# Turning the last context tile in the middle of the second chunk of the second layer's input stage

## The reference

```python
h = rmsnorm(x, p["g_pre_mix"]) * (1 + sc1) + sh1
hc = rmsnorm(xc, p["g_pre_mix"]) * (1 + sc1c) + sh1c
u = h @ w_in
if last:
    uc_mla_kv = hc @ w_in[:, MLA_Q_END:MLA_KV_END]
    uc_na_kv = hc @ w_in[:, NA_Q_END:]
...
y_cf = conformer_conv_mixer(u[..., MLA_KV_END:CF_END], ...)
```

## Time and profile before

| | us |
|---|---|
| median of 3 runs | 1428.51 (1427.56 to 1429.23) |
| the profiled execution | 1429.31 |
| its span, first to last instruction | 1427.4 |
| TensorE busy | 1388.3 (97% of the span) |
| VectorE, ScalarE, GpSimd busy | 994.5, 672.1, 83.3 |
| mean granted TensorE clock | 0.998 of full speed |

### The profile page before, as it was taken

How to read it: one execution, slowest core, us unless ns; L and a number is a source line. 1 busy time by engine, 2 the same in 40 slices (tenths; PEclk the granted TensorE clock), 3 DMA queues, 4 the chain that set the end, 5 groups by cost and what they waited for, 6 DMA issues and landing times.

```text
span 1427.4 us, 21688 instructions
## 1 busy us (share of the span) xinstructions
PE 1388.3 (97%) x8558; PEld 1188.3 (83%) x8558; DVE 994.5 (70%) x1507; ACT 672.1 (47%) x1057; POOL 83.3 (6%) x125
## 2 busy tenths in 40 slices
PE   6999999999999999999999999999999999999998
PEld 3787657888888888788868899888998999899996
DVE  3777477567776856678785765567897556786867
ACT  4421366651231313456266644466545664654544
POOL 0000000010001111100000360000000000000000
PEclk9999999999999999999999999999999999999999
DMA  9422460343645647436322455555545434455453
GB/s 384 192 74 74 177 237 31 140 170 107 233 163 200 227 162 287 155 118 215 116 73 99 169 190 192 180 201 197 175 178 177 153 129 169 156 178 186 169 207 118
DMA packets 39510, 241.06 MB, mean 169 GB/s; under 512 B 4496, under 2 KB 4928, under 8 KB 15488
## 3 DMA queue, kind: packets, MB, share of 16 engines
q1 hardware_dynamic: 28624, 198.92, 38.3%
q0 software_dynamic: 10800, 40.92, 8.2%
HBM read 238.75 MB, written 1.07 MB: 168 GB/s over the span
## 4 chain that ended last, share of the span: by engine, by line
PE 86%; DVE 5%; DMA 4%; ACT 4%; issue 1%; SPq 0%; DVEq 0%; ACTq 0%; POOLq 0%
PE ps L662 44%; PE ps L711 17%; PE ps L743 5%; DMA w<-in_stream 3%; PE ps L630 2%; PE ps L682 2%; PE ps L771 2%; DVE w_lo L486 2%; PE ps L1159 1%; PE ps L799 1%; PE ps L1039 1%; PE ps L1192 1%; DMA U<-in_start 1%; ACT w_hi L476 1%; PE ps L854 1%
## 5 line engine op out<-in xcount | busy, mean ns | idle before, releaser
L662 PE MATMUL ps<-h_hi,w_hi 128*128 128x256 f32 (+1 forms) x1488 | 464.3, 312 | 2.6 <-DVE w_lo L486 1.4
L662 PE MATMUL ps<-h_hi,w_lo 128*128 128x256 f32 (+1 forms) x1488 | 460.2, 309 | 0.0
L662 PE MATMUL ps<-h_lo,w_hi 128*128 128x256 f32 (+1 forms) x1488 | 460.1, 309 | 0.0
L486 DVE TENSOR_TENSOR w_lo<-w,w_hi 128x1024 fp32r<-128x1024 f32 x332 | 393.1, 1227 | 73.4 <-ACT w_hi L476 69.3
L476 ACT ACTIVATE w_hi<-w 128x1024 fp32r<-128x1024 f32 x332 | 333.0, 1053 | 226.6 <-DMA w<-in_stream 226.5
L662 PEld LDWEIGHTS ps<-h_hi,w_hi 128*128 128x128 f32 x1488 | 283.9, 191 | 20.4 <-issue 3.7
L662 PEld LDWEIGHTS ps<-h_lo,w_hi 128*128 128x128 f32 x1488 | 283.9, 191 | 14.9 <-issue 0.5
L662 PEld LDWEIGHTS ps<-h_hi,w_lo 128*128 128x128 f32 x1488 | 283.8, 191 | 14.6
L711 PE MATMUL ps<-w_hi,g_hi 128*128 128x512 f32 x344 | 134.9, 392 | 1.7 <-DVE w_lo L486 1.0
L711 PE MATMUL ps<-w_hi,g_lo 128*128 128x512 f32 x344 | 133.9, 389 | 0.0
L711 PE MATMUL ps<-w_lo,g_hi 128*128 128x512 f32 x344 | 133.9, 389 | 0.0
(11 more groups left out here) (336 smaller groups left out, 1962.6 us busy)
## 6 DMA issues: line engine op xcount, KB each, us to landing
w<-in_stream SPq DMA_DIRECT2D x176, 1024.0 KB, 4.8
hf<-in_mod_blocks POOLq DMA_DIRECT2D x38, 512.0 KB, 4.2
SW<-in_mod_blocks POOLq DMA_DIRECT2D x18, 512.0 KB, 4.9
U<-in_start SPq DMA_DIRECT2D x4, 1024.0 KB, 16.0
GA<-gates POOLq DMA_DIRECT2D x6, 512.0 KB, 4.7
w<-in_start SPq DMA_DIRECT2D x2, 1024.0 KB, 9.8
w<-in_stream SPq DMA_DIRECT2D x4, 512.0 KB, 7.3
GA<-in_start SPq DMA_DIRECT2D x2, 1024.0 KB, 10.9
```

The lines of the kernel that those rows point to most:

```text
L486: dve.tensor_tensor(k.w_lo[:, c.slot, half], k.w[:, c.slot, half], k.w_hi[:, c.slot, half].bitcast(f32), ALU.subtract).then_inc(k.lo_done, 1)
L662: last = pe.matmul(k.banks(2 * c.pair, n, j * (512 if tiles == 2 else n)), w[a][:, c.slot, at:at + 128], h[b][:, kt * stride:kt * stride + n],
```

## The change

In the second layer alone, the turning of tile 3 is taken from between chunk 0 and chunk 1 and is made the `middle` of chunk 1, between its first 24 and its last 24 matmuls.

```diff
     middle = {4: latent_squares, 9: lambda: scores(1)}
+    if l == 1:
+        middle[1] = lambda: pe_tile(k, pe, "mix1", 3)
...
             to_features(k, pe, At(c0 + j), h, KT, 256, 2, n, NT_ALL, before_kt=tokens_ready.get(j), middle=middle.get(j))
-        if l == 1 and j == 0:
-            pe_tile(k, pe, "mix1", 3)
         if j in after:
             after[j]()
```

## The result

The changed kernel takes 1433.67 us (median of 12 runs, 1431.67 to 1436.98), the kernel before 1428.62 us (12 runs, 1427.44 to 1430.83). The ratio is 1.0033, with a 95% interval from 1.0026 to 1.0041: slower by 5 us, and the whole interval is above the 0.2% that the prediction took as its line. The forecast was 1431.6 us in a range from 1429.4 to 1433.9; the measured time is in the range, and 0.4 us from what the clock rival gave (1433.3). It is 2.1 us above the forecast itself.

A forecast was written before the change was run, and what follows sets the result against it. TensorE, 86% of the chain, bounds the kernel. Chunk 2 starts 3.05 us late (0.95 us transposes, 2.10 us new wait), so the median goes from 1428.51 to about 1431.6 us; range 1429.4 to 1433.9 us.

The forecast's parts named there:

- the clock rival: TensorE's idle stretches of 2.61 and 2.1 us halve its clock, up to 1.7 us more: 1433.3 us; chance 0.20.
- Part 1: Chunk 1's first matmul still waits for `w_lo` from VectorE; two waits become one of 2.61 us; gain 0.
- Part 2: Transposes inside chunk 1 lose their cover and take 0.95 us of TensorE's time among dense matmuls.
- The sum: Span 1427.4 + 3.05 = 1430.45 us; median of the runs from 1428.51 to 1431.56, say 1431.6 us (+0.21%).
- Part 3: ScalarE's and VectorE's work queued behind the turned tile makes chunk 2 start at 654.52, not 651.47: +3.05 us.
- Part 4: After chunk 2 no later wait up to 735 us absorbs the delay, so nothing gives the 3 us back.
- the likeliest case: The forecast itself, 1431.6 us from chunk 2's start 3.05 us later; chance 0.56.

The follow-up runs named there:

- e6: Changed kernel with the first half of chunk 1's `w_lo` made ahead of the norm of tile 3; 1432.68 us, ratio 1.0025 to the kernel before.
- e5: Changed kernel, chunk 0's take and chunk 2's weight split put ahead of tile 3's work on ScalarE and VectorE, idle stretch before chunk 1 filled; 1430.14 us, ratio 1.0010.
- e4: Kernel before, transposes in their old place, only the signal to ScalarE moved to after the 24th matmul of chunk 1; 1433.24 us, ratio 1.0030.
- e2: Changed kernel with unused transposes filling TensorE's idle stretches, 20 ahead of chunk 1 and 16 ahead of chunk 2; 1432.90 us, ratio 1.0028.
- e1: The changed kernel run once more with nothing filled; 1436.03 us, ratio 1.0038 to the kernel before.
- e3: Changed kernel with only the idle stretch ahead of chunk 1 filled, by 20 unused transposes; 1433.25 us, ratio 1.0030.
- e8: Changed kernel with only the idle stretch ahead of chunk 2 filled, by 16 unused transposes; 1433.76 us, ratio 1.0029.
- e7: Changed kernel, chunk 1's weights split ahead of tile 3's norm, chunk 2's split and chunk 0's take ahead of tile 3's reads, nothing filled; 1428.09 us, ratio 0.9994.
- e12: Version of e7 with ten unused transposes right ahead of the first layer's 1.46 us wait; 1426.41 us, ratio 0.9979 to the kernel before.
- e10: Changed kernel with both idle stretches filled and ten unused transposes in the first layer, one step behind its wait; 1433.27 us, ratio 1.0032.

## Why the prediction was right, and where it was not

**Part 1 (chunk 1's start does not move): right.** The wait was 2.52 us (2.61 expected), released by `w_lo`, and e6 shows that this `w_lo` was its cause.

**Part 2 (0.95 us for the transposes): right in size, wrong as a term of a sum.** e5 measures 0.86 us. But e4 shows that taking them off the path doesn't save them: the start of chunk 2 moves by 2.58 us with them covered (e4) and by 3.09 with them in the chain (e2). The step of the prediction that wrote the 3.05 as "0.95 is the work of the transposes and 2.10 a new wait" is right as a description of TensorE's time and misleading as a price list. The sum itself was not made that way, but along the chain, and held.

**Part 3 (chunk 2 starts 3.05 us later): right.** At full clock (e2) it was 3.09, with ScalarE idle for 5.03 us ahead of its reads, where about 5 was forecast. The lag from VectorE's first half of `w_lo` to TensorE was 1.47 us in the changed kernel in place of the 1.36 taken from chunk 1.

**Part 4 (it stays): right.** L1105 had no wait, VectorE's idle time behind it was 2.51 us (2.48 in rows 7), and at 742.89 us the delay of 7.72 us was whole. Its steps are to be seen in e2, since in the changed kernel's trace the second fall holds TensorE back, and VectorE waits for it at the take of `q` (0.42 us). In e2 VectorE takes `q` at 672.59; counted from the last matmul of chunk 0 this is 3.75 us later than before, where the prediction has 3.81. ScalarE's squares end 0.93 us before TensorE wants them, where it has 0.8; it gives no working for their start, 672.65.

**The chances: the likeliest case was the wrong one.** Three of the twelve runs, 1431.67, 1431.76 and 1431.81 us, lie at the forecast of 1431.6 us, with a mean granted clock of 0.998 or 0.999. Four lie at 1433.6 to 1434.6 (0.997, one 0.998), two at 1432.7 (0.998), and the slowest three, 1436.36 to 1436.98, have 0.996. The prices of a fall (1.5 and 1.7 us) and these clocks fit no further fall in the changed stretch in the fastest runs, one in the middle and two in the slowest. Only the profiled runs show where their falls lie, so for the others this is an inference; a run without the fall at 227 us and with one in chunk 1 would be hard to tell from the forecast. The prediction gave the clock 0.20, for one fall. That was too little by the rows it had itself: rows 9 show a fall after TensorE had been busy for 0.79 of 2.60 us, and the change made one stretch of 2.61 us with nothing in it and a second of 2.1. The weak step is "at 643.03 it was busy for 1.06 of 2.61 us, and the clock stayed": it describes the stretch filled with the very transposes that the change takes out. The prediction says in the next sentence that emptying it brings it below the gap at 224.6 us, and still leaves the chance at 0.20. The price of 1.7 us was right. The count of one fits the median run, and not the profiled one, which had two.

**How much of it was luck.** The cost in the queues, 3.05 us, was worked out and is confirmed. That the median came to lie in the range was not: it hangs on how many runs of a set have one fall or two. The same kernel in e1 has a median of 1436.03 us over five runs, 6.5 us above the kernel before beside it and outside the range. The high end of the range held only one fall, and 3 of 12 and 3 of 5 runs have the clock of three, the one at 227 us among them.

The Trainium skill (TensorE: Matmul & The Clock Gate, HAM oscillation) warns of idle gaps of TensorE, and draws the line at gaps longer than these. The traces differ: the clock fell after waits of 2.52 and 2.14 us in the changed kernel, and around one of 1.46 us in the first layer.

## What to carry to other kernels

Before moving a step behind some work to fill a wait, look at what released the wait (here `w_lo`, from a queue that the move doesn't touch) and at every in-order queue that stands behind the step's signal: a step that looks free on its own engine may be the start signal of two others. Here the step alone was 0.9 us of work, and the late signal made 3.1 us of it. A wait of 2 us on TensorE costs more than 2 us when the clock falls behind it (here 1.5 to 1.7 us more); count such stretches, one by one, and expect the time to vary from run to run. Where a wait can't be removed, unused transposes in it can hold the clock (e2, with C where the sum puts it), if the timeline shows that they stand ahead of the wait and not behind it.

## What was not expected of the hardware

A fall of the granted clock to half lasted 3.4 to 3.6 us each time (227.2 to 230.8 us before, 648.2 to 651.6 and 658.3 to 661.7 us after) and cost 1.5 to 1.7 us on the path. The same wait had it in one execution and not in another: ahead of chunk 2 the clock fell behind 2.15 us in e1 (0.77 from 655 to 660 us) and not behind 2.14 us in e3 (1.00); and at 227 us, where the order of work is the same in all of them, it fell before, after and in e1 to e4 and e8, and stayed at 1.00 in e5, e6 and e7. What decides between the two is not shown. Part of the spread of this kernel, 3.8 us between runs of the kernel before on the chip of e12, goes with it, as the clocks of the single runs show. Not all of it does: e2 had the gap at 227 us unfilled, a fall there in its trace, and a spread of 0.9 us, and e10 has 2.4 us at one and the same mean clock.
